# mLSTM layer of a streaming encoder: gate rows spread over the partitions by DMA from a DRAM scratch, instead of by products with the identity

## What is computed

```python
b = jnp.cumsum(lfc, axis=-1)                                   # log forget gates, summed in the chunk
log_d = jnp.where(causal, b[..., :, None] - b[..., None, :] + igc[..., None, :], NEG)
s_hat = jnp.einsum('cbhik,cbhjk->cbhij', qc, kc) * jnp.exp(log_d - m_intra[..., None])
...
m_t = jnp.maximum(b_c + m[..., None], mi_c)                    # running maximum, one number per token
num = s_inter[..., None] * jnp.einsum('bhlk,bhkv->bhlv', q_c, C) + s_intra[..., None] * num_c
hcell = num / jnp.maximum(jnp.abs(qn), jnp.exp(-m_t))[..., None]
C = a_old[..., None, None] * C + a_new[..., None, None] * ckv_c
```

## Time and profile before

| | us |
|---|---|
| median of 3 runs | 3458.34 |
| lowest and highest | 3452.13, 3461.75 |
| the profiled execution, its own time | 3459.31 |
| its span in the profile | 3457.6 |
| mLSTM heads, first `rows_of` to the last of DVE's work | 2077.2 to 2519.9 |
| PE busy over the span | 3205.4 (93%) |

### The profile page before, as it was taken

One profiled execution on the slowest core, in us unless ns is written; L12 is line 12 of the kernel. 1 busy time (PEld: TensorE's weight loads), 2 busy tenths in 40 slices (PEclk: granted clock), 3 DMA queues, 4 the chain that ended last, 5 costly groups with the idle time before them and its releaser, 6 DMA issues. The chain is left out here.

```text
span 3457.6 us, 56187 instructions
## 1 busy us (share of the span) xinstructions
PE 3205.4 (93%) x20698; PEld 3103.9 (90%) x20698; DVE 1484.5 (43%) x2856; ACT 859.7 (25%) x1809; POOL 1209.3 (35%) x1042
## 2 busy tenths in 40 slices
PE   5999999999985999999999979999859999999998
PEld 5889889888875999999999969999859999999997
DVE  4465556555543443333333343334325333333334
ACT  2343443443343121110111124444422110111012
POOL 3333333233313534434443152131153434443430
PEclk8999999999987999999999989999979999999999
DMA  3000100100002111111111020010031111111111
GB/s 128 25 10 25 28 21 8 28 22 9 20 3 77 56 43 55 42 49 37 54 43 48 25 69 20 20 38 20 14 112 43 44 48 38 53 45 46 39 34 50
DMA packets 206958, 137.46 MB, mean 40 GB/s; under 512 B 32121, under 2 KB 198833, under 8 KB 206577
## 3 DMA queue, kind: packets, MB, share of 16 engines
q1 hardware_dynamic: 206832, 135.63, 13.5%
HBM read 120.98 MB, written 14.63 MB: 39 GB/s over the span
## 5 line engine op out<-in xcount | busy, mean ns | idle before, releaser
L89 PE MATMUL ps<-act_hi,ffn_hi 128*128 128x352 f32 x2496 | 813.3, 326 | 60.8 <-POOL ffn_lo L145 59.1
L91 PE MATMUL ps<-act_hi,ffn_lo 128*128 128x352 f32 x2496 | 806.9, 323 | 0.0
L90 PE MATMUL ps<-act_lo,ffn_hi 128*128 128x352 f32 x2496 | 806.0, 323 | 0.0
L143 POOL TENSOR_TENSOR ffn_hi<-ffn_stage,one 128x512 fp32r<-128x512 f32 x296 | 319.4, 1079 | 1034.2 <-PE ps L91 898.5
L89 PEld LDWEIGHTS ps<-act_hi,ffn_hi 128*128 128x128 f32 x2496 | 472.5, 189 | 65.6 <-issue 54.0
L90 PEld LDWEIGHTS ps<-act_lo,ffn_hi 128*128 128x128 f32 x2496 | 474.1, 190 | 0.6
L91 PEld LDWEIGHTS ps<-act_hi,ffn_lo 128*128 128x128 f32 x2496 | 472.6, 189 | 0.0
L145 POOL TENSOR_TENSOR ffn_lo<-ffn_stage,ffn_hi 128x512 fp32r<-128x512 f32 x296 | 406.4, 1373 | 23.2
L900 POOL TENSOR_TENSOR gdn_mt_level<-gdn_mt,joins 128x384 f32<-128x384 f32 x168 | 178.4, 1066 | 595.9 <-DVE gdn_qd L1339 304.7
L730 DVE TENSOR_TENSOR x<-x,ps 128x352 f32<-128x352 f32 x528 | 273.2, 521 | 212.9 <-PE ps L91 212.9
L90 PE MATMUL ps<-ffn_hid_lo,ffn_hi 128*128 128x352 f32 x1056 | 341.7, 324 | 0.0
(11 more groups left out here) (296 smaller groups left out, 5393.3 us busy)
## 6 DMA issues: line engine op xcount, KB each, us to landing
ffn_stage<-in_ffn_w_gu SPq DMA_DIRECT2D x88, 512.0 KB, 3.9
ffn_stage<-in_ffn_w_down SPq DMA_DIRECT2D x44, 512.0 KB, 3.5
gdn_stage<-in_gdn_w_in SPq DMA_DIRECT2D x32, 512.0 KB, 4.3
x_kept<-x SPq DMA_DIRECT2D x2, 4224.0 KB, 12.7
x<-x_kept SPq DMA_DIRECT2D x6, 1408.0 KB, 7.6
ml_stage<-in_ml_w_in SPq DMA_DIRECT2D x16, 512.0 KB, 4.5
load_rows<-in_x_prompt SPq DMA_DIRECT2D x8, 512.0 KB, 4.6
ffn_stage<-in_gdn_w_out SPq DMA_DIRECT2D x8, 512.0 KB, 4.3
```

Source lines behind the costliest of these rows:

```text
L89: pe.matmul(out, w_hi, rhs_hi, start=first, stop=False)
L90: pe.matmul(out, w_hi, rhs_lo, start=False, stop=False)
L91: return pe.matmul(out, w_lo, rhs_hi, start=False, stop=last)
L143: nc.gpsimd.tensor_tensor(hi, st, one, ALU.mult).then_inc(self.hi_done, 1)
```

## The change

The prologue gets three more steps: PE transposes quantities 1 and 2 of all heads and chunks (72 rows) into PSUM, and DVE copies them to SBUF. SP stores them to a DRAM scratch `rows_dram`. From there ACT loads, three chunks at a time, the peak rows into `pe_exp` and the floor rows into `floor`, each by one DMA that repeats 3 rows of 512 B on 128 partitions (196,608 B). Both `rows_of` on PE are gone, and so are PE's waits for `qsc_done`, `e_done` and `floor_done`. ACT and DVE read the rows from SBUF. `floor` has three slots in place of two, `pe_exp` one as before.

```diff
+        rows_dram = nc.dram_tensor("ml_gate_rows", (TILES, HEADS, 2, P), F32).ap()
...
             weights(0, 1, 0)
+            sp.wait_ge(pro.step, 59)
+            sp.dma_start(rows_dram.rearrange("c h q p -> (c h) q p"), pro.rows[:]).then_inc(rows_stored, 16)
...
                 if r > 0:
                     pe.wait_ge(tok_done, t * 6 + 2 * r)
-                rows_of(2, 1, r)
                 if r > 0:
                     pe.wait_ge(made, t * 6 + 2 * r)
...
-                if r > 0:
-                    pe.wait_ge(floor_done, t * 3 + r)
-                rows_of(4, 2, r)
...
                 pieces(2)
-                pe.wait_ge(qsc_done, t * 3 + (r + 1))
-                pe.wait_ge(e_done, t * 3 + (r + 1))
...
+            def rows_of(h, q, r):
+
+                return rows_dram[3 * r:3 * r + 3, bass.ds(h, 1), q].rearrange("c a p -> a c p").to_broadcast([P, BATCHES, P])
+
+            def peaks(h, r):
+                act.sem_inc(ws.act_checked, 1)
+                nc.scalar.dma_start(pe_exp[:], rows_of(h, 0, r)).then_inc(peak_in, 16)
+
+            def floors(h, r):
+                act.sem_inc(ws.act_checked, 1)
+                nc.scalar.dma_start(floor[:, r], rows_of(h, 1, r)).then_inc(floor_in[r], 16)
+
+            def prepare(t, r, pieces, more):
...
-                act.wait_ge(prep_done, t * 15 + (5 * r + 1))
+                act.wait_ge(peak_in, t * 48 + (16 * r + 16))
...
                 nc.scalar.copy(v_tok[:, par, :, 0:DV], grid(2)).then_inc(tok_done, 1)
+                if r < 2 or more:
+                    act.wait_ge(made, t * 6 + (2 * r + 1))
+                    peaks(t, r + 1) if r < 2 else peaks(t + 1, 0)
+                if r == 2 and more:
+                    act.wait_ge(den_done, t * 9 + 3)
+                    floors(t + 1, 0)
...
+                        if (r, i) == (3, 0) and more:
+                            act.wait_ge(den_done, t * 9 + 6)
+                            floors(t + 1, 1)
...
                 act.wait_ge(num_done, t * 9 + 9)
                 act.wait_ge(den_done, t * 9 + 9)
+                if more:
+                    floors(t + 1, 2)
...
+            act.wait_ge(rows_stored, 16)
+            peaks(0, 0)
+            for r in range(BATCHES):
+                floors(0, r)
...
+        pe.wait_ge(step, 56)
+        pe.transpose(ps[0:R, 4, 0:P], flat(gates[:, 1]), tk.ident[:])
+        pe.transpose(ps[0:R, 5, 0:P], flat(gates[:, 2]), tk.ident[:]).then_inc(step, 1)
...
+        do(58, cp, rows[:, 0], ps[0:R, 4, 0:P])
+        do(59, cp, rows[:, 1], ps[0:R, 5, 0:P])
+        dve.wait_ge(step, 59)
```

More of the change, by code:

```diff
@@ L1609, in mlstm_phase @@
         q_scale = buf("q_scale", [P, BATCHES, P], F32)
-        floor = buf("floor", [P, 2, BATCHES, P], F32)
+        floor = buf("floor", [P, BATCHES, BATCHES, P], F32)
         pt = buf("pt", [P, 2, BATCHES, P], F32)
@@ L1640, in mlstm_phase @@
         o_normed, final_done, m_out = sem("o_normed"), sem("final_done"), sem("m_stored")
+        rows_stored, peak_in, floor_in = sem("rows_stored"), sem("peak_landed"), [sem(f"floor_landed{r}") for r in range(BATCHES)]
         block = ctx.enter_context(nc.Block())
@@ L1727, in piece @@
                     mm.then_inc(unit_done, 1)
[L1729 to L1735, removed]
             def prepare(t, r, pieces):
@@ L1857, in prepare @@
                     c = 3 * r + i
-                    op = nc.scalar.activation(q_scale[:, i], ps[:, 2, i * P:(i + 1) * P], ACT.Exp,
+                    op = nc.scalar.activation(q_scale[:, i], pe_exp[:, i], ACT.Exp,
                                               bias=hg[:, 4, c:c + 1], scale=-1.0)
@@ L1862, in prepare @@
                 nc.scalar.activation(pe_exp[:], pe_exp[:], ACT.Exp, scale=-1.0).then_inc(exp_done, 1)
-                act.wait_ge(prep_done, t * 15 + (5 * r + 3))
+                act.wait_ge(floor_in[r], t * 16 + 16)
                 if r == 2:
-                    act.wait_ge(den_done, t * 9 + 3)
                     act.wait_ge(chain, t * 18 + 6)
-                nc.scalar.activation(floor[:, par], grid(4), ACT.Exp, scale=-1.0).then_inc(floor_done, 1)
-                act.wait_ge(prep_done, t * 15 + (5 * r + 4))
+                nc.scalar.activation(floor[:, r], floor[:, r], ACT.Exp, scale=-1.0).then_inc(floor_done, 1)
+                act.wait_ge(prep_done, t * 9 + (3 * r + 2))
                 for i in range(BATCHES):
@@ L1873, in prepare @@
                 pieces(2)
[L1874 removed]
+                act.wait_ge(prep_done, t * 9 + (3 * r + 3))
                 nc.scalar.copy(v_tok[:, par, :, 0:DV], grid(2)).then_inc(tok_done, 1)
+                if r < 2 or more:
[4 more added lines that the diff above has]
+                    floors(t + 1, 0)
             def chunk(t, r, i):
@@ L1894, in head @@
                     if r < BATCHES:
-                        prepare(t, r, pieces)
+                        prepare(t, r, pieces, more)
                     for i in range(BATCHES):
@@ L1941, in prepare @@
                     c = 3 * r + i
-                    op = nc.vector.scalar_tensor_tensor(out=pe_exp[:, i], in0=ps[:, 2, i * P:(i + 1) * P],
+                    op = nc.vector.scalar_tensor_tensor(out=pe_exp[:, i], in0=pe_exp[:, i],
                                                         scalar=hg[:, 0, c:c + 1], in1=tk.later_neg[:],
@@ L1946, in prepare @@
                 dve.wait_ge(exp_done, t * 3 + (r + 1))
-                dve.wait_ge(prep_done, t * 15 + (5 * r + 2))
+                dve.wait_ge(prep_done, t * 9 + (3 * r + 1))
                 if r == 2:
@@ L1965, in chunk @@
                 part = den[:, c * P:(c + 1) * P]
-                nc.vector.scalar_tensor_tensor(out=part, in0=ps[:, 7, 0:P], scalar=-1.0, in1=floor[:, par, i],
+                nc.vector.scalar_tensor_tensor(out=part, in0=ps[:, 7, 0:P], scalar=-1.0, in1=floor[:, r, i],
                                                op0=ALU.mult, op1=ALU.max).then_inc(negative_done, 1)
@@ L1994, in head @@
                         if more and (r, i) == (2, 2):
-                            dve.wait_ge(prep_done, t * 15 + 15)
+                            dve.wait_ge(prep_done, t * 9 + 9)
                             take_raw(t + 1, 0)
@@ L2102, in tensor @@
                   start=True, stop=True).then_inc(step, 1)
+        yield
+        yield
+        yield
+        pe.wait_ge(step, 56)
+        pe.transpose(ps[0:R, 4, 0:P], flat(gates[:, 1]), tk.ident[:])
+        pe.transpose(ps[0:R, 5, 0:P], flat(gates[:, 2]), tk.ident[:]).then_inc(step, 1)
     def do(act, n, *args, **kw):
@@ L2162, in vector @@
         do(56, ts, gates[:, 3], gates[:, 3], MDK ** -0.5, None, ALU.mult)
-        dve.wait_ge(step, 56)
+        do(58, cp, rows[:, 0], ps[0:R, 4, 0:P])
+        do(59, cp, rows[:, 1], ps[0:R, 5, 0:P])
+        dve.wait_ge(step, 59)
     pro = Parts()
     pro.sync, pro.gpsimd, pro.tensor, pro.scalar, pro.scalar_last = sync, gpsimd, tensor, scalar, scalar_last
-    pro.vector, pro.w_split, pro.ab_done, pro.step = vector, w_split, ab_done, step
+    pro.vector, pro.w_split, pro.ab_done, pro.step, pro.rows = vector, w_split, ab_done, step, rows
     return pro
```

2 lines of the change are left out of this document (removed).

## The result

The changed kernel takes 3492.18 us (median of 4 runs, 3489.54 to 3493.93) against 3455.54 us for the kernel before: a ratio of 1.0103, 95% interval 1.0085 to 1.0122. It is slower by some 36 us. The forecast was 3456.0, with a range up to 3470.

A forecast was written before the change was run, and what follows sets the result against it. PE was taken to bound the loop; savings of 3.1, 2.4 and 8.0 us against costs of 1.8 (crowding), 8.4 (clock), 0.4, 0.3 and 0.3 gave -2.3 us from 3459.31, a median of 3456.0, range 3444 to 3470.

The follow-up runs named there:

- e2: The changed kernel without row loads inside its loop, all batches reading the rows of head 0, batch 0: 3437.15 us, ratio 0.9943.
- e3: The changed kernel with three peak-row buffers instead of one, each loaded a head ahead: 3440.23 us, ratio 0.9957.

## What to carry to other kernels

A broadcast load is not priced by its bytes: look for a row with the same source pattern, and where there is none, work out what happens at twice the upper end, too. Issue such a load a full turn ahead of its use; a single buffer that is refilled just behind its last reader puts the whole landing time on the engine that waits, and on everybody queued behind it. And before a transfer is moved earlier, ask which engine it sets loose, and beside what: an early weight load cost 23 us until POOL was told to wait.

## What the runs showed of the hardware

- Reads of the same few DRAM rows by all 128 partitions went at 85 to 87 a microsecond, whether of 512 or 1536 bytes, in one DMA or in three, at a busy share of the 16 DMA engines of 0.19 to 0.40; reads of 512 bytes from distinct addresses of another tensor at 361, with 0.71. Why is open: the runs tell the source from the size, the shape and the queue, not repeated addresses from the place of the scratch, nor one part of the memory path from another.
- DVE operations with both inputs in SBUF took 2.0 to 2.8 times as long beside POOL's split (0.58 to 1.38 and 1.61 us, 0.53 to 1.06), three of them in a row 3.48 instead of 0.88 us. With one input in PSUM the same three kept 0.87 us beside it.
- A gap of 1.88 us on PE was followed by a granted clock of 0.57 and one of 1.89 us by 1.00, so the size of the gap alone does not tell (both e2). Whether such gaps are why the runs of e2 and e3 lie 15 and 32 us apart is not shown: the kernel before, without them in the loop, has runs 13 us apart.
